# Turned blocks of the banded half beside one step of the second dilated stage: a change of order in a two-layer encoder kernel

## What is computed

```python
def token_mixer(h, w_in, sink, g_oa, g_ob, w_out, cos, sin):
    ...
    oa, _ = banded_attention(qa, ka, va, WINDOW_A, S, sink)
    oa = rms_norm(oa.reshape(n, S, D_A).astype(h.dtype), g_oa)
    ...
    ob = dilated_mixture(qb, kb, vb)
    ob = rms_norm(ob.reshape(n, S, D_B).astype(h.dtype), g_ob)
    return jnp.concatenate([oa, ob], axis=-1) @ w_out
```

## Time and profile before

| | us |
|---|---|
| median of 3 runs | 2294.83 (2293.78 to 2295.69) |
| the profiled execution | 2295.82 |
| span of its profile | 2294.0 |
| PE busy in it | 2194.8 |
| POOL busy | 787.3 |
| DVE busy | 1134.4 |
| ACT busy | 631.9 |

### The profile page before, as it was taken

The page is one execution under the profiler, slowest core; times in us unless marked ns, Lnnn a source line. Parts: engine busy times, 40 slices in busy tenths (PEclk is TensorE's granted clock), DMA queues, the critical chain, the costliest instruction groups (busy, mean ns, idle before and its releaser), DMA issues. The chain is left out here.

```text
span 2294.0 us, 35862 instructions
## 1 busy us (share of the span) xinstructions
PE 2194.8 (96%) x13528; PEld 1928.1 (84%) x13528; DVE 1134.4 (49%) x2157; ACT 631.9 (28%) x1562; POOL 787.3 (34%) x442
## 2 busy tenths in 40 slices
PE   7999989999999999999998999999999999999997
PEld 7889877888888888888898888789878888888885
DVE  3575655536555145325355766454465532542353
ACT  3445454234311011001044454443242110110002
POOL 3311202441344444444331111034323444444443
PEclk9999989999999999999999999799999999999998
DMA  6200021321122211222241000122111122222222
GB/s 214 71 19 29 29 74 36 93 74 34 51 65 64 64 62 58 64 64 64 65 147 38 29 29 28 65 83 67 62 38 56 57 63 64 64 64 64 64 64 84
DMA packets 41988, 144.86 MB, mean 63 GB/s; under 512 B 4880, under 2 KB 5136, under 8 KB 41616
## 3 DMA queue, kind: packets, MB, share of 16 engines
q1 hardware_dynamic: 34560, 119.02, 16.7%
q10 hardware_dynamic: 7312, 24.21, 3.0%
HBM read 133.78 MB, written 9.44 MB: 62 GB/s over the span
## 5 line engine op out<-in xcount | busy, mean ns | idle before, releaser
L751 POOL CAST w_hi<-w_landed_tile 128x1024 fp32r<-128x1024 f32 x216 | 225.1, 1042 | 1468.7 <-PE ps L798 1456.6
L798 PE MATMUL ps<-x_turned,w_hi 128*128 128x512 f32 (+1 forms) x3072 | 666.7, 339 | 3.6 <-DVE regions L1470 1.9
L798 PEld LDWEIGHTS ps<-x_turned,w_hi 128*128 128x128 f32 x3072 | 523.0, 188 | 106.5 <-issue 5.5
L798 PE MATMUL ps<-w_hi,x_turned 128*128 128x256 f32 (+1 forms) x2304 | 546.9, 320 | 17.3 <-ACT scratch L1224 12.0
L753 POOL TENSOR_TENSOR w_lo<-w_landed_tile,w_hi 128x1024 fp32r<-128x1024 f32 x216 | 554.6, 2567 | 17.3
L798 PEld LDWEIGHTS ps<-w_hi,x_turned 128*128 128x128 f32 x2304 | 390.9, 193 | 42.6 <-issue 9.3
L798 PE MATMUL ps<-x_turned,w_lo 128*128 128x512 f32 (+1 forms) x1536 | 394.3, 338 | 0.0
L798 PE MATMUL ps<-w_hi,regions 128*128 128x512 f32 (+1 forms) x1312 | 374.5, 369 | 0.0
L798 PE MATMUL ps<-w_lo,x_turned 128*128 128x256 f32 (+1 forms) x1152 | 359.6, 312 | 0.0
L798 PEld LDWEIGHTS ps<-w_hi,regions 128*128 128x128 f32 x1312 | 238.7, 188 | 42.0 <-issue 0.7
L1274 ACT ACTIVATE scratch<-scratch 128x768 f32<-128x768 f32 x44 | 37.3, 848 | 839.1 <-DVE scratch L1540 839.1
(11 more groups left out here) (93 smaller groups left out, 2106.6 us busy)
## 6 DMA issues: line engine op xcount, KB each, us to landing
w_landed_tile<-weights_dram SPq DMA_DIRECT2D x216, 512.0 KB, 3.5
x_hbm<-x_residual ACTq DMA_DIRECT2D x2, 3072.0 KB, 14.4
x_residual<-x_hbm ACTq DMA_DIRECT2D x4, 1536.0 KB, 8.4
rows<-mem_in_dram ACTq DMA_DIRECT2D x8, 512.0 KB, 4.5
scratch<-mem_in_dram ACTq DMA_DIRECT2D x8, 512.0 KB, 6.5
x_residual<-x_in_dram SPq DMA_DIRECT2D x12, 256.0 KB, 5.8
gain<-gains_dram ACTq DMA_DIRECT2D x3, 512.0 KB, 15.4
out<-x_residual ACTq DMA_DIRECT2D x6, 256.0 KB, 3.7
```

What stands on the lines that cost most here:

```text
L751: nc.gpsimd.tensor_copy(W_HI[:, s, :], W_IN[:, s, :]).then_inc(w_rounded, 1)
L798: ins = pe.matmul(dst, lhsT, rhs, start=start, stop=stop, skip_group_check=True)
```

## The change

The turned blocks and the reload of x are all woven beside step 36 instead of steps 36, 37 and 38, and the list of projection blocks and other items is woven beside steps 37 to 49 instead of 39 to 49. The items themselves stay the same, and so do their numbers of instructions.

```diff
@@ -319,8 +319,8 @@
     oa = [[("square", "oa", t)] for t in range(NT)] + [[("rstd", "oa", part)] for part in range(4)]
     items += weave(steps[a:b - 1], spread(oa, third[SOONER:], 3))
     turned, beside = beside_last_stage()
-    items += weave(steps[b - 1:b + 2], turned)
-    items += weave(steps[b + 2:], beside)
+    items += weave(steps[b - 1:b], turned)
+    items += weave(steps[b:], beside)
 
     turn = [("t", "mem", b, half) for b in range(NM) for half in range(2)]
```

## The result

The changed kernel takes 2307.11 us (median of 7 runs, 2302.40 to 2310.85), the kernel before 2295.69 beside it (7 runs, 2293.78 to 2299.77). The ratio is 1.0046, with a 95% interval of 1.0031 to 1.0060: slower by some 10.6 us (7 to 14). The profiled execution took 2308.36 us, 12.5 more than that of before.

What follows compares the result with a forecast made beforehand. TensorE, busy 96% of the span, was taken to bound the kernel, so only its waits and low-clock time count. Waits and early start gave +2.4 us, clock falls 5.1: +7.5, forecast 2302.3 us, range 2296 to 2308.

Steps and rivals of the forecast that it cites:

- "worse" rival: Clock stays low longer in step 37 or after step 41 or 43, two more 5 us stretches: +12, 2307 us; chance 0.15.
- walk along PE: Step-by-step timing of PE from 299.91 in layer 0: 98.0 us a layer, together +2.4 us without the clock's answer.
- clock's answer: Falls to 1.2 GHz after the four long PE waits in steps 41 and 43 of both layers; priced at 5.1 us.
- keep wait: Steps 41 and 43: next group's first block waits for ACT to empty its PSUM banks; 2.7 us lost, twice a layer.
- faster rival: Keeps and adds come in time, keep done about 3.2 us into steps 41 and 43: -12.0, 2283 us; chance 0.08.
- add wait: Steps 45 and 47: next block waits for DVE's add behind the normalise, starting at 3.8 not 2.4; 1.4 us lost, twice.
- queues: Reload of x and memory loads issued sooner, POOL's weight splits as before: costed at nothing, bound 8.4 us.
- three falls of four: Clock falls after three of the four keep waits of about 2.5 us idle, 1.7 us each, 5.1 in all.
- the clock stays up: Rival: the waits come but the clock does not fall behind them; +2.4, 2297.2 us; chance 0.27.
- gain of the early start: Step 37: projection begins at 316.9, clock returns after about 2.4 us at 319.3, 3.4 us sooner in layer 0.
- +7.5: Forecast total over both layers: +2.4 us from the walk along PE plus 5.1 us from the clock's falls.
- that -1.0: Layer 1's term: 98.0 us against 98.96 before, as the clock comes back earlier than its long low run did.

Runs made afterwards that it cites:

- experiment 3: Changed kernel plus nine unread 512-column matmuls before each of the two projection blocks a layer that wait for a keep; 2304.52 us, ratio 1.0023 to the kernel before.
- experiment 4: Changed kernel with the dilated half's sum of squares moved on ACT to the end of its step, behind the keep; 2297.71 us, ratio 1.0000 to the kernel before.
- experiment 2: Changed kernel's early start, but projection blocks dealt two to a step over steps 37 to 48, group boundaries between steps; 2279.36 us, ratio 0.9917 to the kernel before.
- experiment 1: First half of the change on the kernel before: all turned blocks beside step 36, projection still from step 39; 2303.65 us, ratio 1.0014.
- experiment 6: Kernel before with its old start (projection from step 39) but blocks dealt in pairs over ten steps, last four beside step 49; 2287.07 us, ratio 0.9957.
- experiment 8: experiment 2 with the first two projection blocks moved into step 36 among the turned blocks, the rest dealt in pairs; 2269.83 us, ratio 0.9889 to the kernel before.
- experiment 5: Changed kernel run and profiled once more, no edit; 2310.32 us, ratio 1.0051 to the kernel before.

## Why the prediction was right, point by point

The forecast was 2302.3 us, slower, by waits that take the place of others and by the clock. The runs gave 2307.11, inside the range, and slower. By the number alone that is the "worse" rival's 2307 rather than the forecast's 2302.3; the traces decide between them, and no rival's mechanism held.

**The walk along PE.** Lengths in us, predicted and measured (from the start of a step's scores to that of the next step's; step 36 from its first turned block):

| step | predicted, clock's answer apart | layer 0 | layer 1 |
|---|---|---|---|
| 36 | 10.9 | 11.06 | 11.06 |
| 37 | 9.0 | 8.87 | 9.02 |
| 38 | 6.4 | 6.41 | 6.40 |
| 39 | 8.1 | 8.12 | 8.12 |
| 40 | 6.8 | 6.97 | 6.96 |
| 41 | 9.3 | 10.86 | 10.89 |
| 42 | 6.4 | 6.39 | 6.41 |
| 43 | 9.1 | 10.57 | 10.65 |
| 44 | 6.0 | 6.05 | 6.03 |
| 45 | 6.1 | 6.18 | 6.18 |
| 46 | 4.7 | 4.69 | 4.72 |

All but 41 and 43 are within 0.2 us. Those two are over by 1.5 to 1.6, which is the fall of the clock: experiment 3 brought step 41 back to 9.32 by keeping PE busy alone.

**The keep wait.** Keep predicted 5.07 us after the start of step 41, measured 5.06 (342.99 to 348.05). Next block predicted 5.9 after, measured 5.80. The square ahead of the keep is shown to be 0.8 us of the wait: moving it (experiment 4) took that off each. The other 1.6 to 1.7 us are ACT's casts and exponentials, right behind which the keep then started; no run moved those. The faster rival needed the keep to be done 3.2 us after the step's start; even without the square it only began at 4.24.

**The add wait.** Predicted 1.4 us lost, about 1.2 of it as idle; the idle time measured 1.19 and 1.24. No experiment moved the add alone; in experiment 2 these waits went together with the others.

**The queues.** The forecast cost them at nothing, and they cost PE nothing: in neither stretch of the kernel after did PE wait for a DMA or for POOL.

**The clock.** This was the open term: three falls of four at 1.7 us, 5.1 in all. It was four of four, twice, at 1.5 to 1.6, so 6.1 us. The rival "the clock stays up" fell with that, and with it the rule that the forecast cites for it: these gaps are shorter than those it warns of, and the clock fell at all eight. The trace now holds rows that were missing before: at gaps of 2.40 to 2.51 us between dense matmuls the clock fell eight times of eight, at 1.59 to 1.70 (experiment 4) none of four (two in each layer), at 1.07 to 1.24 never in these stretches. The Trainium skill (TensorE: Matmul & The Clock Gate, section "A second HAM failure mode: psum-queue depth-cycling") tells of a kernel in which short waits between groups of matmuls, with PSUM banks used in turn, make the clock swing; the waits of 2.4 to 2.5 us here did so, those of 1.2 us did not. That three of four was so near was in part luck. Of the two gaps that the forecast weighed it by the earlier trace rows, the same trace has each once more in layer 1, the other way round: no fall at 1.51 us (to 1288.09) and one at 1.57 us (to 1240.62). The "worse" rival did not hold either: each new run at the low level ended after 3.4 us. In step 43 PE worked in 3.1 us of it, which at half pace is the 1.5 to 1.6 us that each cost; the forecast's price of 1.7 was near.

**The gain of the early start.** Predicted clock's return in layer 0 at 319.3; it came 2.2 us after the start of the first projection block, at about 318 (the stretch itself began 1.2 us sooner in this execution). The step behind it, that 2.4 us of projection matmuls bring the clock back, was read off layer 1 alone and is no rule. In layer 0 of the same trace the clock came back 4.7 us before the first projection block (rows in the last section), and in experiment 1 0.6 us after it (333.25 to 333.83). That the size came out so well is in part luck.

**What was mis-sized.** The sum was +7.5 and the two stretches together gave +9.7. The term that was off is the count of falls ("I take three falls out of four"): the excess of steps 41 and 43 over the walk is 3.0 us in layer 0 and 3.1 in layer 1, 6.1 where 5.1 stood. The rest is the walk, which came out 0.4 us longer in layer 0 (101.46 - 3.0 = 98.4 instead of 98.0) and 0.6 in layer 1. The other weak step is that -1.0 itself. It priced the 30.5-us low-clock run of one execution as if it belonged to the kernel before; experiment 6 ended it after 20.5 with the same order. With 20.5 there, layer 1 would have had nothing to gain back and the sum would have been some 4 us higher. The profiled execution was no unlucky one, though: its mean granted clock was 0.984, and of the 42 runs of the kernel before beside the experiments 41 had that or less. Time multiplied by granted clock is 2256 to 2260 us in all 42, so their spread from 2290 to 2305 us is time at the low level. Where in those runs it stood is not on record. The remaining 2.9 us of the profiled difference lie outside the stretches, where the ten executions differ by up to 8 us among themselves.

## What to carry to other kernels

When woven work is spread over other steps, look where each group's last item and the next group's first one land: if both fall into one step, the engine that must empty their shared bank has to do it behind all that step's other work, and dealing the work so that every boundary lies between two steps (experiment 2) turned the same early start from 0.5% slower into 0.8% faster. Price a gap on TensorE twice, once as idle time and once by the clock behind it; shortening a gap (experiment 4) can save more than the time taken off the gap. Where a chain over three engines makes TensorE wait at every turn, put dense matmuls that are needed anyway into those waits (experiment 8).

## What the runs showed of the hardware that was not expected

Each gap of 2.4 to 2.5 us between dense matmuls, eight of eight in two profiles, cost another 1.5 us by the clock; the four gaps of 1.6 to 1.7 us in experiment 4 cost only themselves. They do not show a safe length. PE has a gap of 1.51 us at the same place of each layer, in code that no edit here touched, and over the ten profiles the clock fell at it in 10 of 20 cases. The kernel after shows both. PE's timeline and busy time by stretch, layer 0, first profile:

```profile
155.84 0.39 PE L798 MATMUL ps<-w_hi,x_turned 128*128 128x256 f32 x1 [1.51 <-ACT scratch L1224]
155.84:159.24 3.40, 3.40 (x29) 3.40 (x30) 2.29 (x5) 2.41 (x8) 0.00 (x0) 1.00 0.57 159
```

and second profile (experiment 5):

```profile
155.76 0.53 PE L798 MATMUL ps<-w_hi,x_turned 128*128 128x256 f32 x1 [1.51 <-ACT scratch L1224]
155.90:159.20 3.30, 3.30 (x16) 3.30 (x17) 2.33 (x6) 2.27 (x8) 0.00 (x0) 0.50 0.44 158
```

So at that length neither the gap nor the program around it settles whether the clock falls: the same kernel does both. What differs between the executions was not found.

Six 512-column matmuls among the turned blocks (experiment 8) ended a low-clock run after 6.8 us, in both layers; in the other orders without filling it lasted 17 to 31 us. They are not the only thing that ends one. In layer 0 of the kernel before the clock came back at 322.8, behind values, scores and transposes, and the first projection block came only later; both layers of experiment 6 did the same. Busy time by stretch and PE's timeline of the kernel before:

```profile
322.80:327.46 4.66, 4.47 (x36) 3.78 (x37) 2.48 (x6) 2.58 (x8) 0.00 (x0) 1.00 0.37 111
327.46 0.48 PE L798 MATMUL ps<-w_hi,x_turned 128*128 128x512 f32 x1
```

Layer 1 ran the same order and stayed low for 10 us more, until 2.4 us into its projection blocks. What ends such a run is not settled by these runs.

DVE slowed down beside POOL. In experiment 3 the normalise took 1.05 us instead of 0.42, and the scale 3.38 instead of 1.28. The scale began at 365.89 and POOL's subtraction ended at 368.18; the 1.09 us from there to the scale's end is about what it takes alone, so the row looks like a full stop until POOL was done, not like a slower pace. The Trainium skill (SBUF — State Buffer, section "SBUF: two separate sides") says that the two engines share a pair of ports which one of them holds for a whole instruction; the trace agrees with that. In the kernel after POOL had its turn to be slow: its cast at 357.62, begun beside a scale that ran from 357.35 to 358.62, took 1.90 us, the one at 367.05, with DVE idle, 1.04. In experiment 3 a weight split that starts 3 us sooner in its step therefore delayed a keep on ACT, which waits for neither engine's data but stands behind a square that does.
